# The recurrent scan of a two-block transformer kernel: another order of TensorE's products per tile, and three products on GpSimd instead of VectorE

## The reference, cut to what matters

```python
def wkv7_scan(S0, r, decay, kk, b, k, v, reverse, emit):
    def step(S, inp):
        r_t, w_t, kk_t, b_t, k_t, v_t = inp
        sa = jnp.einsum('bhvk,bhk->bhv', S, -kk_t)
        S = S * w_t[:, :, None, :] + sa[..., None] * b_t[:, :, None, :] + v_t[..., None] * k_t[:, :, None, :]
        y = jnp.einsum('bhvk,bhk->bhv', S, r_t) if emit else None
        return S, y

# in rwkv_output, with k_sum the keys of both directions summed:
bonus = jnp.sum(r * k_sum * r_k, axis=-1, keepdims=True) * v
```

## Time and profile before

| | us |
|---|---|
| median of 3 runs | 4389.38 |
| lowest, highest | 4387.12, 4395.81 |
| the profiled execution | 4392.67 |
| its span, first to last instruction | 4390.9 |
| the scan stage in it | about 2860 to 3415 |

### The profile page before, as it was taken

One profiled execution on the slowest core, in us unless ns is written; L12 is line 12 of the kernel. 1 busy time (PEld: TensorE's weight loads), 2 busy tenths in 40 slices (PEclk: granted clock), 3 DMA queues, 4 the chain that ended last, 5 costly groups with the idle time before them and its releaser, 6 DMA issues. The chain is left out here.

```text
span 4390.9 us, 79510 instructions
## 1 busy us (share of the span) xinstructions
PE 3919.1 (89%) x33222; PEld 3243.3 (74%) x33222; DVE 2663.4 (61%) x4533; ACT 1722.4 (39%) x3046; POOL 381.3 (9%) x459
## 2 busy tenths in 40 slices
PE   8998888988999998799578999979999597999997
PEld 6887656877786776587466877778888476888886
DVE  3346658875775655888455014668778644565656
ACT  3037526763564542577446112223222122222222
POOL 0000101210000000121000000033333000000002
PEclk9999988998999999899789999989999798999998
DMA  3111349982000024999310211000000230111110
GB/s 116 39 57 46 107 190 362 395 317 89 15 2 1 1 83 154 362 395 347 130 21 24 93 48 54 21 10 4 3 4 4 103 134 29 58 39 58 39 53 39
DMA packets 174673, 444.09 MB, mean 101 GB/s; under 512 B 29572, under 2 KB 83724, under 8 KB 149740
## 3 DMA queue, kind: packets, MB, share of 16 engines
q1 hardware_dynamic: 165100, 405.44, 24.5%
q0 software_dynamic: 9216, 33.56, 3.0%
HBM read 385.36 MB, written 53.49 MB: 100 GB/s over the span
## 5 line engine op out<-in xcount | busy, mean ns | idle before, releaser
L583 PE MATMUL psum<-weight_parts,h_parts 128*128 128x512 f32 (+2 forms) x2880 | 601.5, 371 | 23.5 <-DVE h_parts L784 14.8
L583 PEld LDWEIGHTS psum<-weight_parts,h_parts 128*128 128x128 f32 x2880 | 508.0, 191 | 110.9 <-DVE h_parts L784 16.6
L1906 DVE TENSOR_TENSOR weight_parts<-weights_raw,weight_parts 128x2048 fp32r<-128x2048 f32 x192 | 432.0, 2288 | 68.5 <-ACT weight_parts L1875 67.2
L1875 ACT ACTIVATE weight_parts<-weights_raw 128x2048 fp32r<-128x2048 f32 x192 | 360.6, 1919 | 100.0 <-DMA weights_raw<-in_moe_w_up 43.8
L1812 PE MATMUL psum<-weight_parts,picked_parts 128*128 128x512 f32 x1536 | 362.0, 395 | 9.2 <-DVE picked_parts L1893 9.2
L2385 PE MATMUL psum<-h_parts,up_parts 128*128 128x512 f32 x1536 | 355.2, 392 | 11.0 <-DVE up_parts L2466 11.0
L2401 PE MATMUL psum<-down_parts,hidden_parts 128*128 128x512 f32 x1536 | 353.5, 391 | 6.7 <-DVE down_parts L2471 6.7
L2385 PEld LDWEIGHTS psum<-h_parts,up_parts 128*128 128x128 f32 x1536 | 291.2, 190 | 72.7 <-DVE up_parts L2466 11.8
L1812 PEld LDWEIGHTS psum<-weight_parts,picked_parts 128*128 128x128 f32 x1536 | 288.9, 190 | 72.4 <-DVE picked_parts L1893 12.4
L2401 PEld LDWEIGHTS psum<-down_parts,hidden_parts 128*128 128x128 f32 x1536 | 290.1, 189 | 67.6 <-DVE down_parts L2471 7.1
L769 DVE TENSOR_TENSOR weight_parts<-weights_raw,weight_parts 128x512 fp32r<-128x512 f32 (+4 forms) x78 | 102.7, 1349 | 379.0 <-ACT weight_parts L652 378.9
(11 more groups left out here) (474 smaller groups left out, 7140.2 us busy)
## 6 DMA issues: line engine op xcount, KB each, us to landing
weights_raw<-in_moe_w_gate SPq DMA_DIRECT2D x64, 1024.0 KB, 13.7
weights_raw<-in_moe_w_up SPq DMA_DIRECT2D x64, 1024.0 KB, 14.2
weights_raw<-in_moe_w_down SPq DMA_DIRECT2D x64, 1024.0 KB, 12.8
w_ada<-in_w_ada SPq DMA_DIRECT2D x12, 2048.0 KB, 8.9
up_raw<-in_w_mlp_up SPq DMA_DIRECT2D x16, 1024.0 KB, 7.4
down_raw<-in_w_mlp_down SPq DMA_DIRECT2D x16, 1024.0 KB, 5.2
weights_raw<-in_even_w_in SPq DMA_DIRECT2D x10, 1024.0 KB, 5.1
weights_raw<-in_w_in SPq DMA_DIRECT2D x10, 1024.0 KB, 5.5
```

Of the source, the lines that this page charges most:

```text
L583: last = pe.matmul(ps[:, t, 0:width(n)], cols[:, i, KP * h + k, t * P:(t + 1) * P], part[:, n % 2, j, k, 0:width(n)], start=(h == 0 and m ...
L1875: act.activation(part[:, n % PART_SLOTS, 0], raw[:, n % RAW_SLOTS], ACT.Copy).then_inc(high, 1)
L1906: dve.tensor_tensor(part[:, n % PART_SLOTS, 1], raw[:, n % RAW_SLOTS], part[:, n % PART_SLOTS, 0].bitcast(F32), ALU.subtract).then_inc(low, 1)
```

## The change

On TensorE, phase 6: the keys-times-values product comes first, then the bonus product (from phase 24, now into columns 256 to 259 of bank B), then the turns. The wait for GpSimd's end-scaled tiles (`ends_scaled`) stands behind the keys-times-values product. Phase 24 ends with y. ScalarE's copy of `L_k_v` takes the four bonus columns along (260 columns with the sign turned, into a tile that `L_k_v` and `a_state` now share), still behind its copy of the turned rows; VectorE subtracts them from `bonus_rows` in phase 13, behind the fourth masking. GpSimd forms receptance times exponential in phase 3, and the first block of the inverse in phase 6 (two products with a wait on its own semaphore between them); VectorE keeps the transpose of that block. TensorE waits for `r_scaled` too before the pairs.

```diff
--- before.py
+++ after.py
@@ -2751,8 +2751,8 @@
         b.X = c.at("below_diagonal", H + 6, [P, 4, 32])
         b.XW = c.at("below_diagonal_wide", WIDE + n, [P, 4, 64])
         b.tm = c.at("b_and_k_rows", H + 6.5, [P, 2, 256])
-        b.LKV = c.at("L_k_v", H + 8.5, [P, 4, 64])
-        b.Z = c.at("a_state", H + 9.5, [P, 4, 64])
+        LZ = c.at("L_k_v_and_a_state", H + 8.5, [P, 8, 64])
+        b.LKV, b.Z, b.LB = LZ[:, 0:4], LZ[:, 4:8], LZ[:].rearrange("p h n -> p (h n)")
         b.U = b.LKV
         b.S = c.at("state", H + 10.5, [P, 3, 2, 64])
         b.SG = c.at("state_decayed", H + 12, [P, 2, 64])
@@ -2860,8 +2860,8 @@
     first_half = lambda d: slice(32 * d, 32 * d + 32)
     second_half = lambda d: slice(32 - 32 * d, 64 - 32 * d)
     names = ("lora_done", "tanh_done", "log_ready", "running_ready", "exps_ready", "key_scaled", "key_ready", "scaled",
-             "ends_scaled", "pairs_done", "pairs_masked", "bk_turned", "bk_copied", "lkv_done", "lkv_copied",
-             "mt_ready", "m_ready", "x_done", "x_masked", "x_wide_cleared", "m_done", "a_state_done", "z_ready",
+             "ends_scaled", "r_scaled", "near_ready", "pairs_done", "pairs_masked", "bk_turned", "bk_copied", "lkv_done", "lkv_copied",
+             "bonus_added", "mt_ready", "m_ready", "x_done", "x_masked", "x_wide_cleared", "m_done", "a_state_done", "z_ready",
              "u_done", "u_ready", "decayed", "s_done", "state_ready", "y_started", "y_done", "tile_done", "state_cleared")
     both = [f"{n}_{i}" for i in range(4) for n in names]
     with stage(nc, "dve_step", "lora_loaded", "tables_loaded", *both) as (
@@ -2899,6 +2899,7 @@
                     for _ in range(4):
                         yield
 
+                    pe.wait_ge(s["r_scaled"], i + 1)
                     pe.wait_ge(s["scaled"], i + 1)
                     for kind, key in ((0, b.bt), (1, b.kt)):
                         for jj in (0, 1):
@@ -2911,20 +2912,24 @@
                     last.then_inc(s["pairs_done"], 1)
                     yield
                     yield
-                    pe.wait_ge(s["ends_scaled"], i + 1)
                     pe.wait_ge(s["pairs_masked"], i + 1)
-                    for n, src in enumerate((b.bb, b.kb)):
-                        for jj in (0, 1):
-                            col = n * 256 + jj * P
-                            last = pe.transpose(ps[:, A, col:col + P], src[:, jj], c.ident[:])
-                    last.then_inc(s["bk_turned"], 1)
                     for par, jj in HEADS:
                         h = 4 * g + 2 * jj + par
                         for cc, C in CH:
                             last = pe.matmul(ps[C, B, slot(par, jj) * 64:(slot(par, jj) + 1) * 64],
                                              b.LL[C, par, 1, jj, 0, :], v_rows(C, t, slice(h * 64, h * 64 + 64)),
                                              start=True, stop=True)
+                    pe.wait_ge(s["ends_scaled"], i + 1)
+                    if emit:
+                        for jj in (0, 1):
+                            last = pe.matmul(ps[:, B, 256:260], b.rk[:, jj], rks[:, 2 * g + jj, 4 * g:4 * g + 4],
+                                             start=(jj == 0), stop=(jj == 1))
                     last.then_inc(s["lkv_done"], 1)
+                    for n, src in enumerate((b.bb, b.kb)):
+                        for jj in (0, 1):
+                            col = n * 256 + jj * P
+                            last = pe.transpose(ps[:, A, col:col + P], src[:, jj], c.ident[:])
+                    last.then_inc(s["bk_turned"], 1)
                     yield
                     pe.wait_ge(s["bk_copied"], i + 1)
                     for level in range(5):
@@ -3003,11 +3008,9 @@
                                     out = ps[C, A + par, 128 + jj * 64:128 + (jj + 1) * 64]
                                     pe.matmul(out, b.LL[C, par, 0, jj, 1, :], b.U[C, slot(par, jj)],
                                               start=False, stop=False)
-                                    pe.matmul(out, b.LL[C, par, 1, jj, 1, :], v_rows(C, t, slice(h * 64, h * 64 + 64)),
-                                              start=False, stop=(jj == 1))
-                        for jj in (0, 1):
-                            last = pe.matmul(ps[:, A, 384:388], b.rk[:, jj], rks[:, 2 * g + jj, 4 * g:4 * g + 4],
-                                             start=(jj == 0), stop=(jj == 1))
+                                    last = pe.matmul(out, b.LL[C, par, 1, jj, 1, :],
+                                                     v_rows(C, t, slice(h * 64, h * 64 + 64)),
+                                                     start=False, stop=(jj == 1))
                         last.then_inc(s["y_done"], 1)
                     yield
 
@@ -3039,7 +3042,9 @@
                     act.activation(b.tm[:].rearrange("p a b -> p (a b)"), ps[:, A, :], ACT.Copy)\
                        .then_inc(s["bk_copied"], 1)
                     act.wait_ge(s["lkv_done"], i + 1)
-                    act.activation(flat(b.LKV), ps[:, B, 0:256], ACT.Copy, scale=-1.0).then_inc(s["lkv_copied"], 1)
+                    width = 260 if t >= 2 else 256
+                    act.activation(b.LB[:, 0:width], ps[:, B, 0:width], ACT.Copy, scale=-1.0)\
+                       .then_inc(s["lkv_copied"], 1)
                     for _ in range(11):
                         yield
                     for q, cc in enumerate((0, 1) if d == 0 else (1, 0)):
@@ -3073,13 +3078,25 @@
                     pool.wait_ge(s["key_scaled"], 2 * i + 2)
                     pool.tensor_tensor(b.kd[:], b.kd[:], kts, ALU.mult).then_inc(s["key_ready"], 1)
                     yield
+                    pool.wait_ge(s["exps_ready"], i + 1)
+                    pool.tensor_tensor(b.ar[:, :, 1, :], r_[:, 2 * g:2 * g + 2, tok(t)], b.e1[:], ALU.mult)\
+                        .then_inc(s["r_scaled"], 1)
                     yield
                     pool.wait_ge(s["scaled"], i + 1)
                     pool.tensor_tensor(halves(b.bb), halves(b.bt), end(b.ge[:]), ALU.mult)
                     pool.tensor_tensor(halves(b.kb), halves(b.kt), end(b.ge[:]), ALU.mult)
                     pool.tensor_tensor(b.rk[:], r_[:, 2 * g:2 * g + 2, tok(t)], b.kd[:], ALU.mult)\
                         .then_inc(s["ends_scaled"], 1)
-                    for _ in range(13):
+                    yield
+                    yield
+                    near = masks[d].neighbour_turned[:].unsqueeze(1).unsqueeze(1).to_broadcast([P, 2, 2, 64])
+                    pool.wait_ge(s["pairs_masked"], i + 1)
+                    pool.tensor_tensor(b.MT[:].rearrange("p (a j) n -> p a j n", a=2), b.LL[:, :, 0, :, 0, :], near,
+                                       ALU.mult).then_inc(s["near_ready"], 1)
+                    pool.wait_ge(s["near_ready"], i + 1)
+                    pool.tensor_tensor(b.MT[:], b.MT[:], eye[:].unsqueeze(1).to_broadcast([P, 4, 64]), ALU.add)\
+                        .then_inc(s["mt_ready"], 1)
+                    for _ in range(11):
                         yield
                     for q, cc in enumerate((0, 1) if d == 0 else (1, 0)):
                         ends = b.ge[:].rearrange("p (j q) -> p j q", q=2)[:, :, cc].unsqueeze(2)\
@@ -3108,7 +3125,7 @@
                 mask = masks[d]
                 for i, t in enumerate(tiles_of[d]):
                     emit = t >= 2
-                    kkt, rt = kk[:, pair, tok(t)], r_[:, pair, tok(t)]
+                    kkt = kk[:, pair, tok(t)]
                     yield
                     dve.wait_ge(s["log_ready"], i + 1)
                     way = slice(None) if d == 0 else slice(None, None, -1)
@@ -3124,7 +3141,6 @@
                     edge = 0 if d == 0 else 63
                     dve.tensor_copy(a[:, :, :, edge], kq[:, :, :, edge])
                     dve.tensor_tensor(a[:, :, :, to], kq[:, :, :, to], ex[:, :, :, before], ALU.mult)
-                    dve.tensor_tensor(b.ar[:, :, 1, :], rt, b.e1[:], ALU.mult)
                     step(dve.scalar_tensor_tensor(b.bt[:], b.bt[:], 0.5, b.e3[:], ALU.mult, ALU.mult))
                     dve.wait_ge(s["key_ready"], i + 1)
                     dve.tensor_tensor(b.kt[:], b.kd[:], b.e3[:], ALU.mult).then_inc(s["scaled"], 1)
@@ -3136,11 +3152,6 @@
                                       mask.order[:].rearrange("p a t -> p (a t)").unsqueeze(1).to_broadcast([P, 8, P]),
                                       ALU.mult).then_inc(s["pairs_masked"], 1)
                     yield
-                    dve.wait_ge(s["pairs_masked"], i + 1)
-                    near = mask.neighbour_turned[:].unsqueeze(1).unsqueeze(1).to_broadcast([P, 2, 2, 64])
-                    step(dve.tensor_tensor(b.MT[:].rearrange("p (a j) n -> p a j n", a=2), b.LL[:, :, 0, :, 0, :], near,
-                                           ALU.mult))
-                    dve.tensor_tensor(b.MT[:], b.MT[:], wide(eye[:]), ALU.add).then_inc(s["mt_ready"], 1)
```

(8 more changed lines are left out.)

## The result

The changed kernel is slower: 4402.73 us (median of 20, 4390.97 to 4420.13) against 4393.10 (20 runs beside it, 4381.67 to 4402.98), ratio 1.0027 [1.0018, 1.0037]. The prediction was 4378. The profiled execution took 4402.26 us (span 4400.4) against 4392.67 before.

A forecast was written before the change was run, and what follows sets the result against it. Bound: TensorE up to about 3120.6 of the turn, then VectorE's chain from the scan. Terms −10.6 + 0.5 + 1.65 − 0.5 − 2 = −11 us, clock unchanged; 4392.67 − 11, less 3.3, gives 4378 us, range 4364 to 4389.

The forecast's parts named there:

- in the new rhythm every turn draws a fall: Rival, steady scan turns: each draws a 1.2 us clock fall, where 8 of 28 do now; +13, 4402 us; chance 0.10.
- the term of the clock: Steady scan turns: 0 to 16 falls to the 1.2 GHz level, −10 to +10 us; taken as no change.
- model turn: Scan loop, pair group at 3113.07 to the next at 3126.27: 13.20 us, the turn the per-tile terms were read from.
- Order on TensorE: Keys times values, bonus, then turns: TensorE gains 0.69 − 0.30 = 0.39 us per tile with a bonus.
- changes of tile size that don't vanish: Rival, TensorE: bonus to turns costs 0.3 instead of 0.11 us, only 0.33 − 0.15 left; −5, 4384 us; chance 0.17.
- What reaches the scan: Log decay ready 0.06 us earlier, scan starts 0.20 us earlier, out of TensorE's 0.39.
- ScalarE eats half of it: ScalarE's order of turned rows, L_k_v copy and tanh eats TensorE's gain: 0.20 of 0.39 us arrives.
- The holding: VectorE's rate product held by GpSimd's receptance product: 0 to 0.38 us per tile, 0.15 taken, against 0.33 saved.
- The block: Inverse's first block on GpSimd: ready about 3118.2, 1 us slack, cost 0, nothing gained on the path.
- The sum of the steady turns: 28 scan turns at 0.20 + 0.33 − 0.15 = 0.38 us each: −10.6 us.
- The other turns: Early scan turns: +0.1 in each of 5, about +0.55 in each of 3, −0.5 for the first three.
- The end: Stage's end: last bonus group alone on the path, 1.01 us, and VectorE's sum behind; with two smaller ones about −2 us.

The follow-up runs named there:

- e3: Kernel before with the new TensorE order, bonus and wider copy alone, both products left on VectorE: 4383.55 us, ratio 0.9976 to the kernel before.
- e14: Kernel before with only receptance times exponential moved to GpSimd: 4386.59 us, ratio 0.9973 to the kernel before.
- e11: Changed kernel with receptance times exponential back on VectorE, no filling: 4379.41 us, ratio 0.9955 to the kernel before.
- e1: Changed kernel plus eight unread TensorE products ahead of each of two waits (scaled tiles before the pairs, z of the second chunk): 4366.45 us.
- e4: Kernel before with receptance product and inverse's first block moved to GpSimd, TensorE's order as before: 4381.47 us, ratio 0.9963 to the kernel before.
- e2: Kernel before plus eight unread TensorE products ahead of each of two waits (scaled tiles before the pairs, z of the second chunk): 4382.33 us.
- e15: Changed kernel with ScalarE copying L_k_v before the turned rows, no filling: 4383.46 us, ratio 0.9970 to the kernel before.
- e9: Changed kernel with unread TensorE products ahead of the pairs and z waits in each stream's first two tiles only: 4389.69 us, ratio 0.9982 to the kernel before.
- e12: Changed kernel with the inverse's first block back on VectorE, no filling: 4396.60 us, ratio 0.9994 to the kernel before.
- e13: Changed kernel itself measured once more, nothing altered: 4401.61 us, ratio 1.0017 to the kernel before.
- e7: Changed kernel with one more unread product on VectorE's chain in phase 3, 0.4 us longer: 4445.10 us, ratio 1.0109 to the kernel before.

## Why the prediction was wrong, step by step

It forecast 4378 us and gave 4402 a chance of 0.10. That rival, "in the new rhythm every turn draws a fall", is what happened in kind: 22 of 28 turns, and 14 more falls than before. That its 4402 meets the measured 4402.73 is in part luck. It had 20 more falls at 1.2 us, +24; measured are 12.6 us more lost in the steady turns and 11.5 at the start, which no term had. **The step that failed is the term of the clock.** It read "0 to 16 falls, that is −10 to +10 us; I take no change". The count was 22, outside these bounds, and the clock took 24 us more than before. The evidence I weighed against it, that a less busy stretch had no fall at all, was one sample of another kind of turn; the stretch has 0.86 now, most of it from the late rise, but two falls are in it as well. The 1.2 us for a fall was low too: the model turn of 13.20 is above the mean free turn of 13.11, and by this a fall in before cost 1.5.

It was also argued from one place. The prediction laid the falls to the standstill before the pairs, by the window at 3072. Six of before's eight falls do begin 0.1 to 0.2 us behind a pair group, right behind that standstill; but the one in the window is of the other two. It begins ahead of the standstill, which ends at 3072.66:

```profile
3071.50:3071.75 0.25, 0.25 (x16) 0.25 (x13) 0.25 (x2) 0.00 (x0) 0.00 (x0) 1.00 0.00 0
3071.75:3072.00 0.25, 0.25 (x12) 0.25 (x8) 0.25 (x2) 0.00 (x0) 0.00 (x0) 0.51 0.00 0
```

So there were two kinds of fall to see. The change shortens the pairs' pause (free turns' mean distance between the starts of loads: 0.85 to 0.58 us) and leaves the z pause (0.54 to 0.57); the first kind vanished, and all 22 of after, at 0.9 to 1.5 us ahead of the group, are of the second.

The rest, with the turn at 3113.07 as the model (us behind the pair group):

| step | before | predicted | after, 3261.21 |
|---|---|---|---|
| first load of the turns | 4.51 | 4.73 | 4.69 |
| turned rows' copy | 5.21 | 5.43 | 5.47 |
| L_k_v copy | 5.83 | 6.05 | 5.96 |
| tanh | 6.47 | 6.41 | 6.23 |
| log decay | 7.49 | 7.43 | 7.23 |
| scan | 8.20 | 8.00 | 7.89 |
| next pairs | 13.20 | 12.82 | 12.65 |

- **Order on TensorE: right.** From the inverse step's last load (3264.87) to lora's first it takes 1.70 us, 1.67 predicted, with no gap between bonus and turns. The rival with changes of tile size that don't vanish fell.
- **What reaches the scan: right in kind**, ScalarE does run without idle before the tanh. The size was off: its two copies and the tanh stand 0.49 and 0.27 us apart, where I took 0.62 and 0.36. The scan comes 0.31 earlier, not 0.20, and e3 has 0.38 for the whole turn: about all of TensorE's 0.39, so the step that ScalarE eats half of it is wrong in size.
- **The holding: right.** Groups of the steady turns, before and then after (busy us, mean ns):

```profile
L3119 DVE SCALAR_TENSOR_TENSOR rate<-rate,rwkv_cols 128x256 f32<-128x256 f32 x27 | 10.3, 383 | 0.0
```

```profile
L3136 DVE SCALAR_TENSOR_TENSOR rate<-rate,rwkv_cols 128x256 f32<-128x256 f32 x28 | 15.3, 546 | 0.0
L3082 POOL TENSOR_TENSOR a_and_r<-rwkv_cols,exp_after 128x256 f32<-128x256 f32 x28 | 20.2, 723 | 0.0
```

  0.16 us in the mean, against 0.15 taken; 0.26 in the turn shown. The Trainium skill, page GPSIMD Engine Reference, section Key points, names contention between GpSimd and a VectorE instruction with two SBUF inputs; the trace agrees, 546 against 383 ns, and its GpSimd partner kept its 0.72 us. Alone (e14) the move was worth 0.17, against 0.33 − 0.15 = 0.18 reckoned; on top of the order only 0.05 (12.72 in e11, 12.67 in e1). Why is not shown.
- **The block: right.** It was ready at 5.15 us behind the group, VectorE waited 0.41 us for it in time it had over, and its wait before the state sum grew to 1.15 us, as foretold. Worth nothing: e4 and e14 have the same free turn (12.95).
- **The sum of the steady turns: too small.** 28 × 0.38 = 10.6 predicted, 12.4 measured without falls (e2 to e1), 0.44 a turn. That it comes this close is luck in part: 0.20 for the order and 0.18 for the receptance product stand against 0.38 and 0.05 measured.
- **The other turns: too dear.** +1.65 predicted up to the 12th group, −0.2 measured (137.1 in e2, 136.9 in e1). The end: −2 predicted, −2.2 measured from before to after.

So all terms but one add up to −11 predicted and −12.4 − 0.2 − 2.2 = −14.8 measured, and −15.9 by the medians of e2 and e1. The clock then took 24 us more than before: 24.4 in the steady turns (379.3 − 354.9, 22 falls of 1.1 us) against 11.8 (379.1 − 367.3, 8 falls of 1.5), and some 11.5 at the start against none. −14.8 + 24.1 = +9.3 is nearly the +9.6 of the two profiled executions.

**What stays open.** Why the same pause draws 20 or 22 falls in a turn of 12.66 us and 7 in one of 12.60 (e15) is not settled. The near equality of 13.65 and 13.7 us fits the changed kernel, e9, e12 and e13, but e7 has as many falls without it; the pause at L2957 fits all twelve kernels with an open z pause, but no run changed it alone.

## What to carry to other kernels

Where the granted clock of a stage already shows falls, the number of falls can be a term of the sum as large as the edit, as it was here: slice the windows down to a quarter of a microsecond to find which pause stands ahead of a fall, and price the edit with every turn drawing one. Then close that pause on TensorE itself; eight products that nobody reads, in front of one wait, were worth 31 us here, twice the whole change. Compare two orders with the pauses filled on both sides first, or the clock's answer is taken for the edit's.
